# The product of a chunk's inverse with its right hand sides on four quarters of the array, with a copy across lanes on VectorE

## What is computed

```python
def step(S, inp):
    r, w, k, v, a, b = inp
    sa = jnp.einsum('dbhij,dbhj->dbhi', S, a)
    S = S * w[..., None, :] + sa[..., :, None] * b[..., None, :] + v[..., :, None] * k[..., None, :]
    y = jnp.einsum('dbhij,dbhj->dbhi', S, r) if emit else None
    return S, y
```

## Time and profile before

| | us |
|---|---|
| median of 3 runs | 3436.86 |
| lowest, highest | 3433.54, 3439.82 |
| the profiled execution | 3430.51 |
| its span in the trace | 3428.7 |

### The profile page before, as it was taken

One profiled execution on the slowest core, in us unless ns is written; L12 is line 12 of the kernel. 1 busy time (PEld: TensorE's weight loads), 2 busy tenths in 40 slices (PEclk: granted clock), 3 DMA queues, 4 the chain that ended last, 5 costly groups with the idle time before them and its releaser, 6 DMA issues.

```text
span 3428.7 us, 78520 instructions
## 1 busy us (share of the span) xinstructions
PE 3226.2 (94%) x33764; PEld 2536.4 (74%) x33764; DVE 1506.5 (44%) x2822; ACT 1179.3 (34%) x2499; POOL 826.5 (24%) x518
## 2 busy tenths in 40 slices
PE   7999999999999998999999889999999988989998
PEld 5777777777777787888888666666666666768886
DVE  4446464554354662200044464656564356430033
ACT  4433333433343424311112353343432345342222
POOL 2211111101122232122323221111111233434453
PEclk9999999999999999999999999999999999999999
DMA  5434343344355342122112233323243243523322
GB/s 209 137 98 115 108 129 119 94 125 134 114 173 178 129 165 82 37 66 63 61 50 66 74 108 102 100 75 103 72 116 102 89 131 104 200 73 93 96 92 74
DMA packets 246697, 364.90 MB, mean 106 GB/s; under 512 B 154096, under 2 KB 155376, under 8 KB 245888
## 3 DMA queue, kind: packets, MB, share of 16 engines
q1 hardware_dynamic: 226976, 294.57, 28.5%
q10 hardware_dynamic: 14976, 35.66, 2.7%
q0 software_dynamic: 4448, 30.31, 2.5%
HBM read 291.27 MB, written 69.21 MB: 105 GB/s over the span
## 4 chain that ended last, share of the span: by engine, by line
PE 78%; DVE 7%; issue 3%; ACT 3%; DMA 2%; DVEq 2%; SPq 1%; POOLq 1%; POOL 0%; PEld 0%; ACTq 0%; PEldq 0%
PE banks L279 21%; PE banks L280 18%; PE banks L281 18%; PE banks L1613 2%; PE banks L1624 2%; PE banks L982 2%; PE banks L392 1%; PE banks L1581 1%; PE banks L1637 1%; PE banks L1616 1%; PE banks L1010 1%; DMA slot<-in_w_mix 1%; PE banks L1978 1%; POOLq L2350 1%; DVE arena L594 1%
## 5 line engine op out<-in xcount | busy, mean ns | idle before, releaser
L281 PE MATMUL banks<-hx_rounded,slot_rounded 128*128 128x512 f32 (+1 forms) x1624 | 571.9, 352 | 0.0
L864 POOL TENSOR_TENSOR slot_rounded<-slot,branch_weights_high 128x512 fp32r<-128x512 f32 x188 | 245.2, 1326 | 1349.0 <-ACT branch_weights_high L859 1347.7
L279 PE MATMUL banks<-hx_high,weight_parts 128*128 128x512 f32 (+1 forms) x1512 | 537.7, 356 | 10.9 <-DVE hx_low L542 10.4
L279 PE MATMUL banks<-hx_rounded,branch_weights_high 128*128 128x512 f32 (+1 forms) x1280 | 511.1, 399 | 31.7 <-DVE arena L1325 10.7
L280 PE MATMUL banks<-hx_low,weight_parts 128*128 128x512 f32 (+1 forms) x1512 | 537.6, 356 | 0.0
L281 PE MATMUL banks<-hx_high,weight_parts 128*128 128x512 f32 (+1 forms) x1512 | 535.7, 354 | 0.0
L280 PE MATMUL banks<-resid_rounded,branch_weights_high 128*128 128x512 f32 (+1 forms) x1280 | 449.2, 351 | 0.0
L281 PEld LDWEIGHTS banks<-hx_rounded,slot_rounded 128*128 128x128 f32 x1624 | 309.0, 190 | 43.7
L279 PEld LDWEIGHTS banks<-hx_high,weight_parts 128*128 128x128 f32 x1512 | 286.6, 190 | 54.4 <-issue 13.6
L279 PEld LDWEIGHTS banks<-hx_rounded,branch_weights_high 128*128 128x128 f32 x1280 | 242.7, 190 | 110.7 <-issue 59.7
L281 PEld LDWEIGHTS banks<-hx_high,weight_parts 128*128 128x128 f32 x1512 | 286.0, 189 | 41.2
(11 more groups left out here) (262 smaller groups left out, 5869.7 us busy)
## 6 DMA issues: line engine op xcount, KB each, us to landing
slot<-in_w_mix SPq DMA_DIRECT2D x120, 512.0 KB, 4.1
slot<-in_w_ffn_in SPq DMA_DIRECT2D x88, 512.0 KB, 3.5
arena<-chunk_inputs SPq DMA_DIRECT2D x48, 640.0 KB, 4.2
arena<-in_w_ada SPq DMA_DIRECT2D x50, 512.0 KB, 4.5
slot<-in_w_ffn_out SPq DMA_DIRECT2D x44, 512.0 KB, 3.5
slot<-in_w_ada SPq DMA_DIRECT2D x40, 512.0 KB, 3.9
chunk_inputs<-arena SPq DMA_DIRECT2D x80, 256.0 KB, 3.9
arena<-side_projections POOLq DMA_DIRECT2D x16, 1152.0 KB, 6.5
```

Of the source, the lines that this page charges most:

```text
L279: first = nc.tensor.matmul(out, w_hi, x_hi, start=start, stop=False)
L281: return first, nc.tensor.matmul(out, w_lo, x_hi, start=False, stop=stop)
L864: last = nc.gpsimd.tensor_tensor(slots_r[g % 3][:, half], slots[g % 3][:, half], weights_high(g)[:, half], ALU.subtract)
```

## The change

Step 14 is done in twice as many products of half the width. For each head the state half goes first, for both directions, and lands on the other direction's lanes, in bank C; then the value half, on the own lanes, in bank A. So the four products of a head sit on the four quarters of the array. The state half then lies on the wrong lanes. DVE takes it from there: two copies of 64 lanes and 128 columns for each chunk, each from one half of the lanes to the other, into `ZZ`, where ACT had put it. Step 15 waits for DVE (its 13th result) instead of ACT's third. ACT has five results to a block and chunk instead of six, DVE fourteen instead of thirteen, and the later waits are renumbered. Nothing else moves: the fill, the gaps and the order of the other work are as before.

```diff
@@ -1633,12 +1633,13 @@
                 on_act(j, 2)
                 for h in range(2):
                     for d in range(2):
-                        rows = lanes(d)
-                        last = nc.tensor.matmul(A[j][rows, h * 2 * HD:(h + 1) * 2 * HD], XX[j][rows, h, X1], WR[j][rows, h].rearrange("p o j -> p (o j)"), start=True, stop=True)
+                        nc.tensor.matmul(C[j][lanes(1 - d), h * HD:(h + 1) * HD], XX[j][lanes(d), h, X1], WR[j][lanes(d), h, 0], start=True, stop=True)
+                    for d in range(2):
+                        last = nc.tensor.matmul(A[j][lanes(d), h * HD:(h + 1) * HD], XX[j][lanes(d), h, X1], WR[j][lanes(d), h, 1], start=True, stop=True)
                 step(j, last, 14)
             fill(11)
             for j in range(2):
-                on_act(j, 3)
+                on_dve(j, 13)
                 for d in range(2):
                     for h in range(2):
                         rows = lanes(d)
@@ -1695,10 +1696,9 @@
                 between(i)
             for j in range(2):
                 on_pe(j, 14)
-                zq = A[j][:, 0:4 * HD].rearrange("p (h o j) -> p h o j", h=2, o=2)
-                nc.scalar.activation(ZZ[j], zq[:, :, 0, :], ACT.Copy).then_inc(blk_act[j].sem, 1)
+                zq = A[j][:, 0:2 * HD].rearrange("p (h j) -> p h j", h=2)
                 for d in range(2):
-                    last = nc.scalar.activation(QV[j][lanes(d), d], zq[lanes(d), :, 1, :], ACT.Copy)
+                    last = nc.scalar.activation(QV[j][lanes(d), d], zq[lanes(d)], ACT.Copy)
                 last.then_inc(blk_act[j].sem, 1)
             between(11)
             between(12)
@@ -1758,6 +1758,11 @@
                         x, ps = XX[j][:, :, X1], A[j][:, 4 * CHUNK:6 * CHUNK].rearrange("p (h t) -> p h t", h=2)
                     nc.vector.tensor_tensor(x, x, ps, ALU.add).then_inc(blk_dve[j].sem, 1)
                 between(2 * m)
+            for j in range(2):
+                on_pe(j, 14)
+                for d in range(2):
+                    last = nc.vector.tensor_copy(ZZ[j][lanes(d)], C[j][lanes(1 - d), 0:2 * HD].rearrange("p (h j) -> p h j", h=2))
+                last.then_inc(blk_dve[j].sem, 1)
             between(11)
             for j in range(2):
                 on_pe(j, 15)
```

More of the change, by code:

```diff
@@ L781, in program @@
         staged = Count(sem("chunk_inputs_staged"), HP * NBLK, 16)
-        NPE, NDV, NAC = 16, 13, 6
+        NPE, NDV, NAC = 16, 14, 5
         blk_pe = [Count(sem(f"chunk_products_{n}"), HP * NBLK, NPE) for n in ("even", "odd")]
@@ L1650, in block_pe @@
                 fresh = n == 0 and j == 0
-                on_act(j, 4)
+                on_act(j, 3)
                 for d in range(2):
@@ L1662, in block_pe @@
                 if not (n == 0 and j == 0):
-                    on_dve(j, 13)
-                    pe.wait_ge(blk_act[1 - j].sem, blk_act[1 - j].ready(l, it, 5 - NAC if j == 0 else 5))
+                    on_dve(j, 14)
+                    pe.wait_ge(blk_act[1 - j].sem, blk_act[1 - j].ready(l, it, 4 - NAC if j == 0 else 4))
                     for d in range(2):
@@ L1723, in block_dve @@
             it = hp * NBLK + n
-            A = [bank[3 * j] for j in range(2)]
+            A, C = [[bank[3 * j + x] for j in range(2)] for x in (0, 2)]
             def two(j, x):
```

## The result

| | median us | runs | lowest to highest | profiled execution, its span |
|---|---|---|---|---|
| before | 3437.01 | 14 | 3430.34 to 3441.48 | 3430.51, 3428.7 |
| after | 3443.94 | 14 | 3440.31 to 3448.26 | 3447.61, 3445.8 |

The changed kernel takes 1.002 times the time of the one before, with a 95% interval from 1.0013 to 1.0027: about 6.9 us more. The forecast was 10.9 us less. So the traces are compared in the recurrence, block by block, and the whole by medians.

What follows compares the result with a forecast made beforehand. PE, busy 94% of the span, was taken to bound the kernel. Gains of 10.6, 0.3, 1.6, 1.0 and 2.5 less losses of 4.0 and 1.1 gave 10.9 us less: 3436.9 to 3426.0 us, range 3420 to 3438.

Steps and rivals of the forecast that it cites:

- Step 14, 0.63 us: On PE, the new step on four quarters takes 0.63 us instead of 1.02, saving 18.7 us in 48 blocks.
- the rival without overlap: Products of two row halves into one bank run in turn; step 14 takes 1.22 us; total 3448; chance 0.06.
- Copies 0.30 us apart: DVE's four copies per block do not overlap, because each changes lanes; one starts every 0.30 us.
- The rivals of cheap and of dear copies: Cheap: a copy every 0.20 us, 3422.7, chance 0.17. Dear: 0.42 a copy, 3444.5, chance 0.08.
- The usual block, 0.38: In 28 of 48 blocks the fill hides both chunks' copies, so 0.38 us each is kept: 10.6 us.
- The short fills, the blocks without outputs and the three roundings: Gains: six short-fill blocks 0.05 us each, six without outputs 0.27 each, three with ACT rounding a slab 2.5 together.
- The scan blocks, 1.32 lost each: In three first-layer blocks the copies wait behind DVE's two scans, so step 15's odd chunk starts later: 4.0 us lost.
- The load, 1.1 lost: Three times in the second layer the chain runs through a weight slab's load, losing the neighbouring block's 0.38: 1.1 us.
- It costs nothing there.: DVE's next-gap work behind the copies makes L1765 ready at 3.1, before PE asks at about 3.2: no loss.
- The prediction's last sign: If step 14 takes 0.63 and time exceeds 3434, copies or DVE's work behind them are the cause; PE's waits name it.
- The clock: PE's granted clock was 1.00 in both recurrence stretches; the sum priced no fall.
- The fourth rival: The change works but the end does not move: waits take the gain back; 3434 to 3437; chance 0.06.

Runs made afterwards that it cites:

- both edits: The change plus two order edits: scans L1305 behind GM (first layer), ACT's square L1183 two gaps later (second layer); 3425.07 us, ratio 0.9968; second trace 3424.45, 0.9964.
- the scans moved: The change with one order edit: DVE's scans L1305 moved from gap 10 to gap 12, behind GM, in the first layer; 3437.47 us, ratio 1.0005.
- the one with ACT's copies: The kernel before with the four-quarter step 14 alone; ACT instead of DVE copies the state half across the lanes; 3452.75 us, ratio 1.0043.
- the kernel with the state half on its own lanes: The change with scans and square moved, but step 14's state half on its own lanes (two quarters), one 128-lane DVE copy per chunk; 3436.7 us, ratio 0.9999.
- both edits without the change: The kernel before with only the two order edits, scans L1305 behind GM and square L1183 two gaps later; 3436.01 us, ratio 0.9998.
- the kernel with the other order: The change with scans and square moved, and the odd chunk's two DVE copies in the other order; 3424.39 us, ratio 0.9963.

## Why the prediction was wrong

Point by point, in its order.

- **Step 14, 0.63 us.** Right: 0.62. Two row halves writing one bank did not slow it, so the rival without overlap fell.
- **Copies 0.30 us apart.** Right: 0.31, four in 1.21 or 1.22. The reason given is borne out too: with two neighbours on the same lanes the four take 1.10. With that the Trainium skill (VectorE: DVE Perf Modes, section Two Vector instructions with no wait between them), whose rule is that an instruction which starts in another group of 32 lanes is held until the earlier ones have finished, agrees with these rows. The rivals of cheap and of dear copies did not come about.
- **The usual block, 0.38.** Nearly: 0.32 to 0.33 on average. The odd chunk's copies were to be hidden by 0.03 and are late by 0.06 (step 15 runs 0.73 us instead of 0.67). Blocks with a longer fill keep 0.37 to 0.42.
- **The short fills, the blocks without outputs and the three roundings.** Right in kind and near in size. The short fills gain 0 for 0.05, but for the one at 2660, which loses 0.6: PE waits 0.9 us for DVE behind an operation that took 0.95 us instead of 0.43 (L1743), for a cause that no run shows. The blocks without outputs gain 0.22 to 0.33 for 0.27, the roundings 0.73 for 0.82.
- **The scan blocks, 1.32 lost each.** The wait is right: 1.34 ahead of the even chunk, and step 15 is over 1.42 us later than before. Taking the scans away gave 6.5 us where 4.0 had been priced. In the change each of the three blocks has 3.4 us of half clock, about 1.4 us each. But only one of these stretches begins behind this wait, and eight such stretches are there in the 27 like blocks of the traces without it, so only the 4 us are shown to be the wait's.
- **The load, 1.1 lost.** Not borne out. In the three blocks at 2229, 2398 and 2564 the sum had nothing left over, and the change gains 2.8 us there, the second trace with both edits 2.4. PE's wait at these places is shorter (before, then after):

```profile
PE banks L1667 <- ACT arena L1710: 3.4, 3, 1.5
```

```profile
PE banks L1668 <- ACT arena L1710: 1.6, 2, 1.2
```

  At the third place ACT waits 2.03 us for the slab's load where it waited 2.97. Why the load lands sooner stays open.
- **"It costs nothing there."** This is the step that failed: DVE's work of the next gap behind the copies. I worked out when L1765 would be ready behind it, and asked for no other reader of that work, so the wait that ended up on PE's path was put at nothing. In three blocks of the second layer it is L1282, ACT's L1183 waits for it, and what PE needs, L1701, stands behind L1183 in ACT's queue. Two edits, one on ACT's order and one on DVE's, each take this out, and give 9.5 and 7.0 us. 4.9 us of it are the wait. The prediction's last sign pointed there: with step 14 at 0.63 and the time above 3434, what DVE does behind the copies was to be the cause, and a wait of PE on a line after step 15 was to name it.
- **The clock.** Both stretches had a granted clock of 1.00, and the sum held it there. In the change's recurrence 27.3 us are at 0.50, which at the prices above is some 12 us. For other idle times no run here ties the fall to the wait (see the last section).

**The sum again.** In the recurrence of the two traces the change takes 9.3 us more (711.4 + 619.2 against 706.8 + 614.5), where 10.9 less were forecast: 20.2 us apart. Block by block, from one step 14 to the next, 13.0 of it lie in the three blocks with the wait on L1701 (5 the wait, 8 the clock behind it) and 4.4 in the three with the scans (their clock). 1.8 lie in the block at 545, where PE's L1589 waits 1.62 us for ACT's L1714: ahead of that stands the rounding L859, which waits for its slab's load.

```profile
555.26 1.06 ACT L859 ACTIVATE branch_weights_high<-slot 128x1024 fp32r<-128x1024 f32 x1 [1.64 <-DMA slot<-in_w_mix]
```

Six of the eight traces in which DVE copies across lanes have that wait, of 1.0 to 1.6 us, and the traces of the other four kernels don't; one of the two traces of the kernel with both edits has it and the other hasn't. The other usual blocks make 1.7, mostly by their late odd chunks, all other blocks about 2, and the loads 2.8 the other way. With both edits the forecast's own terms make 16.0 us less (10.9, the scans' 4.0, and 0.38 for each of these three blocks). The second trace has 14.4 us less (701.2 + 605.7), at a clock of 1.00 throughout the recurrence, as before. That they come so near is in part luck, since the loads gave 2.4 that had not been forecast. But most terms that were priced held, and two that were not priced, the wait on L1701 and the clock, turned the sign. The fourth rival had the gain taken back by waits, but argued from PE's busy share against it; a busy share of before says nothing of waits that the change makes.

## What to carry to other kernels

Where an instruction that waits is put into an engine's queue, follow each instruction queued behind it to its readers, and the readers' own queues to whoever stands behind them: here the victim was two queues away, on the engine that the change was meant to relieve. In this kernel work without a deadline did best behind the step that the bounding engine waits for, on both engines. And where a wait is added on a matrix engine that runs at full granted clock, a price for the clock after it belongs into the range.

## What the runs showed of the hardware

- All six waits of 1.63 us on L1701 (three in the change, three with the scans moved) were followed by 3.4 or 6.8 us of granted clock 0.50, which began 0.4 to 1.4 us after PE's next product. In the nine traces of kernels in which PE does not wait there (before, and all others but the one with ACT's copies) no stretch began in the same places behind step 14; one began 0.7 us ahead of it, in the kernel with the state half on its own lanes.
- An idle time alone does not decide it. Before, PE waited for 1.70 us at the third block, and the clock stayed at 1.00. The same wait in the first trace of the kernel with both edits, and in the second (the clock of the first was 0.50 from 235.9 on, that of the second was not):

```profile
235.11 0.35 PE L279 MATMUL banks<-hx_rounded,branch_weights_high 128*128 128x256 f32 x1 [1.70 <-DVE arena L1325]
```

```profile
234.95 0.36 PE L279 MATMUL banks<-hx_rounded,branch_weights_high 128*128 128x256 f32 x1 [1.71 <-DVE arena L1329]
```

```profile
233.44 0.35 PE L279 MATMUL banks<-hx_rounded,branch_weights_high 128*128 128x256 f32 x1 [1.72 <-DVE arena L1329]
```

  What decides between them stays open. This wait of 1.7 us (once 2.1) comes three times in each first layer. In the three traces with the two-quarter step 14 (before, both edits without the change, own lanes) no stretch followed it in nine times; in the six with the four-quarter step and without the waits on the scans one did in eight of eighteen. Whether the denser products of step 14 make the fall more likely is a rival that no run here settles. The second layer's waits behind L1701 don't hang on it: there the same products without the wait had no stretch.
- Four 64x64 records on two quarters take 0.12 us and on four quarters 0.06, and a step of this kind has some 0.13 us besides (worked out from 32 records in 1.08 and 0.62, and 16 in 0.61).
- A DVE copy of 64x128 from PSUM starts 0.31 us after the one ahead when the lanes change and 0.21 when they do not (starts at 348.43, 348.74, 348.95 and 349.24 in the kernel with the other order). With 64x64 copies the second, on the same lanes, starts 0.15 after the first (350.55, 350.70), and the next, on other lanes, 0.23 after the second (350.93). So half the columns save 0.06 and 0.08. ACT's copies across the lanes start 0.29 us apart, and its copies that stay on their lanes (L1701) 0.28 to 0.30.
